# Expert layers: gates applied by one VectorE multiplication per group, normalised one group later

## The reference

```python
def peer_ffn(x, norm_g, q_w, sub_keys, u, v):
    h = rmsnorm(x, norm_g).reshape(T, D)
    q = (h @ q_w).reshape(T, PEER_HEADS, 2, PEER_HALF)
    s = jnp.einsum('thcd,ckd->thck', q, sub_keys)
    s1, i1 = lax.top_k(s[:, :, 0], PEER_TOPK)          # 16 of 128 keys
    s2, i2 = lax.top_k(s[:, :, 1], PEER_TOPK)
    cand_s = s1[..., :, None] + s2[..., None, :]
    best_s, best_pos = lax.top_k(cand_s, PEER_TOPK)    # 16 of 256 pairs
    gate = jax.nn.softmax(best_s, axis=-1)
    a = jnp.einsum('nd,nhkd->nhk', hb, u[ib])          # dot with the gathered row of u
    w = gb * jax.nn.gelu(a, approximate=False)
    return jnp.einsum('nhk,nhkd->nd', w, v[ib])        # sum of the gathered rows of v
```

## Time and profile before

| | |
|---|---|
| median of 3 runs | 2998.92 us (2991.95 to 3008.18) |
| the profiled execution | 2997.89 us, its span 2996.1 us |
| DVE / ACT / PE / POOL busy | 56% / 39% / 85% / 32% of the span |
| first expert layer, first gather to last value matmul | 1414.4 to 2092.2 us |
| second expert layer, the same | 2269.0 to 2946.2 us |
| DMA in most of both | 418 GB/s |

### The profile page before, as it was taken

How to read it: one execution, slowest core, us unless ns; L and a number is a source line. 1 busy time by engine, 2 the same in 40 slices (tenths; PEclk the granted TensorE clock), 3 DMA queues, 4 the chain that set the end, 5 groups by cost and what they waited for, 6 DMA issues and landing times.

```text
span 2996.1 us, 35285 instructions
## 1 busy us (share of the span) xinstructions
PE 2532.5 (85%) x11858; PEld 1798.1 (60%) x11858; DVE 1685.7 (56%) x3591; ACT 1172.0 (39%) x2504; POOL 946.0 (32%) x736
## 2 busy tenths in 40 slices
PE   7999899999789999858888878787877887788787
PEld 7988699899669979737544333233755443333334
DVE  4551355555465534672566766665365666677663
ACT  4446544434464346423333232323453332323233
POOL 0005400000230048226444333332525443333343
PEclk9999999999899999879999999999888999989998
DMA  5553255455325545204999999998417999999993
GB/s 190 183 170 120 96 190 182 165 182 185 107 92 182 189 156 185 68 28 158 393 410 406 422 421 419 419 413 341 155 57 290 416 408 419 421 420 421 414 415 151
DMA packets 141950, 783.39 MB, mean 261 GB/s; under 512 B 15872, under 2 KB 16384, under 8 KB 76288
## 3 DMA queue, kind: packets, MB, share of 16 engines
q0 software_dynamic: 73728, 536.90, 43.5%
q1 hardware_dynamic: 65360, 237.44, 23.6%
q10 hardware_dynamic: 2736, 7.46, 0.8%
HBM read 780.69 MB, written 1.05 MB: 261 GB/s over the span
## 4 chain that ended last, share of the span: by engine, by line
PE 45%; DMA 21%; issue 10%; DVE 10%; POOL 7%; ACT 6%; POOLq 0%; SPq 0%; DVEq 0%; ACTq 0%
DMA arena<-experts,arena 21%; PE ps L451 12%; PE ps L452 11%; PE ps L453 11%; POOL ring_lo L312 5%; PE ps L892 5%; PE ps L895 4%; DVE arena L1908 4%; ACT row L1307 2%; POOL arena L2013 1%; ACT arena L1300 1%; DVE ring_lo L312 1%; DVE arena L1426 0%; DVE hT_lo L1492 0%; POOL rs L1992 0%
## 5 line engine op out<-in xcount | busy, mean ns | idle before, releaser
L892 PE MATMUL ps<-arena,row 128*128 128x512 f32 x1024 | 576.7, 647 | 219.4 <-ACT row L1307 219.3
L1908 DVE SCALAR_TENSOR_TENSOR arena<-arena,ps 128x1024 f32<-128x1024 f32 x512 | 612.1, 1219 | 263.1 <-DMA arena<-experts,arena 263.0
L2013 POOL DMA_INDIRECT arena<-experts,arena x512 | 487.1, 951 | 735.2 <-PE ps L895 527.4
L451 PE MATMUL ps<-hT_hi,ring_hi 128*128 128x256 f32 x2048 | 597.2, 292 | 62.5 <-POOL ring_lo L312 56.5
L452 PE MATMUL ps<-hT_lo,ring_hi 128*128 128x256 f32 x2048 | 592.9, 289 | 0.0
L453 PE MATMUL ps<-hT_hi,ring_lo 128*128 128x256 f32 x2048 | 592.4, 289 | 0.0
L895 PE MATMUL ps<-arena,row 128*128 128x512 f32 x1024 | 559.4, 629 | 0.0
L306 ACT ACTIVATE ring_hi<-ring 128x1024 fp32r<-128x1024 f32 x448 | 462.8, 1057 | 168.9 <-PE ps L453 154.8
L312 POOL TENSOR_TENSOR ring_lo<-ring,ring_hi 128x1024 fp32r<-128x1024 f32 x180 | 433.9, 2418 | 294.0 <-ACT ring_hi L306 232.0
L892 PEld LDWEIGHTS ps<-arena,row 128*128 128x128 f32 x1024 | 198.0, 203 | 514.2 <-ACT row L1307 300.7
L451 PEld LDWEIGHTS ps<-hT_hi,ring_hi 128*128 128x128 f32 x2048 | 406.5, 199 | 71.6 <-issue 65.8
(11 more groups left out here) (261 smaller groups left out, 2941.2 us busy)
## 6 DMA issues: line engine op xcount, KB each, us to landing
ring<-stream SPq DMA_DIRECT2D x448, 512.0 KB, 3.7
arena<-experts,arena POOLq DMA_INDIRECT x512, 13.0
row<-rows_in ACTq DMA_DIRECT2D x11, 512.0 KB, 4.0
x<-x_in SPq DMA_DIRECT2D x1, 1024.0 KB, 5.1
out<-arena SPq DMA_DIRECT2D x2, 512.0 KB, 2.7
arena<-cols_in ACTq DMA_DIRECT2D x3, 256.0 KB, 2.6
cols<-cols_in SPq DMA_DIRECT2D x1, 425.5 KB, 5.6
arena<-cols_in ACTq DMA_DIRECT2D x1, 320.0 KB, 2.9
```

The lines of the kernel that those rows point to most:

```text
L451: pe.matmul(dst, a[0], b[0], start=start, stop=False)
L892: lower = pe.matmul(ps[:, 2 * tb, :], diag, v[:, 0:HALF], start=first, stop=end)
L1908: last = dve.scalar_tensor_tensor(u, u, 1.0, h, ALU.mult, ALU.mult, accum_out=R["a"][:, n % 2, k:k + 1])
L2013: pool.indirect_dma_start(R["held"][:, g % HELD, :], None, experts, bass.IndirectOffsetOnAxis(ap=idx[:, n % 2, k:k + 1], axis=0))\
```

## The change

ACT no longer scales the four numbers of a group. It applies Gelu, raises `peer_g` and waits for `peer_w`. DVE multiplies the group's four Gelu results with its four gates in one instruction (`gated`), which stands two dots into the **next** group (one dot in where that group has two picks, none where it has one), and raises `peer_w`; the layer's last group has its multiplication at the end. The three instructions of `gates(n)` move from the end of unit n - 1 to behind group 0 of unit n; those of unit 0 stay where they were.

```diff
                 def weights(n, group):
                     first, end = groups_of(n)[group]
                     act.wait_ge(of("peer_a"), group_count(l, n, group) + 1)
-                    act.wait_ge(of("peer_gate"), UNITS * l + n + 1)
-                    link(act.activation(R["g"][:, n % 2, first:end], R["a"][:, n % 2, first:end], ACT.Gelu))
-                    for k in range(first, end):
-                        last = act.activation(R["w"][:, n % 2, k:k + 1], R["g"][:, n % 2, k:k + 1], ACT.Copy,
-                                              scale=R["gate"][:, n % 2, k:k + 1])
-                    link(last)
+                    act.activation(R["g"][:, n % 2, first:end], R["a"][:, n % 2, first:end], ACT.Gelu)\
+                       .then_inc(of("peer_g"), 1)
+                    act.wait_ge(of("peer_w"), group_count(l, n, group) + 1)
                     taken = PICKS * l + TOPK * n + end - 2 * GROUP
...
+                def gated(n, group):
+                    first, end = groups_of(n)[group]
+                    dve.wait_ge(of("peer_g"), group_count(l, n, group) + 1)
+                    dve.wait_ge(of("peer_gate"), UNITS * l + n + 1)
+                    dve.tensor_tensor(R["w"][:, n % 2, first:end], R["g"][:, n % 2, first:end],
+                                      R["gate"][:, n % 2, first:end], ALU.mult).then_inc(of("peer_w"), 1)
+
                 def dots(n, group):
                     h = bank(4 + 2 * (n // PH), 2)
-                    for k in range(*groups_of(n)[group]):
+                    first, end = groups_of(n)[group]
+                    for k in range(first, end):
+                        if k == first + min(2, end - first - 1) and (n or group):
+                            gated(*((n, group - 1) if group else (n - 1, len(groups_of(n - 1)) - 1)))
...
                 for n in range(UNITS):
                     dots(n, 0)
+                    if n:
+                        gates(n)
                     if n + 1 < UNITS:
                         top_keys(n + 1)
...
                     for group in range(3, len(groups_of(n))):
                         dots(n, group)
-                    if n + 1 < UNITS:
-                        gates(n + 1)
...
+                gated(UNITS - 1, len(FINE) - 1)
                 add_piece(layer, in_banks, 1)
```

## The result

The changed kernel takes 3015.22 us (median of 20 runs, 2999.93 to 3021.69), the kernel before 3000.52 us in the same rounds (20 runs, 2991.95 to 3008.77). The ratio is 1.0039 with a 95% interval of 1.0028 to 1.0050. On 3000.5 us that is 11.7 us more, between 8.4 and 15.0; the two medians themselves stand 14.7 us apart. The forecast was 11.6 us more, said as 3010 us because the median known then was 2998.9.

What follows compares the result with a forecast made beforehand. The prediction took the gathers' DMA to bound the kernel, leaving only layer starts and ends open. Starts 8.6 plus ends 3.0 gave 11.6 us on 2997.9 us: 3009.5, said as 3010 us, range 2997 to 3024 us.

Steps and rivals of the forecast that it cites:

- The bound: In the picks' stretch DMA gathers limit the time, share 1.01 at 418 GB/s; only places with an empty queue are open.
- The starts, 4.3 us each: At each layer's start the twelfth gather goes out 4.3 us later and nothing makes up for it; 8.6 us in all.
- upper end: At the starts: 5.2 us per layer, if one pick more runs at half clock after TensorE's longer idleness.
- The ends, 1.5 us each: At each layer's end the weights of picks 8 to 11 follow pick 12's dot, 1.5 us later; 3.0 us in all.
- the upper bound: At the ends: 3.2 us each, if picks 4 to 7, also late, run at half clock into this point.
- The picks' stretch, 0: With the picks alone, later slots cost 0: gathers keep at least 7.9 us to land and need 5.2.
- ACT's list, 0: Work behind ACT's wait for the multiplication costs 0; beside queries the nearest gather has 10.9 us against 5.2 needed.
- The multiplication, 0.2 us hidden: On DVE, 66 multiplications per layer at 0.2 us, 26 us in all, hidden in its waits for landings.
- The gates, 0: Moving the gates removes 30 DVE waits of some 4.3 us; gain 0, at most 2 us per layer.
- Nothing is lost at the start: Rival: the start's queue is empty for another reason and the 4.3 us fall into it; 2998 to 3001 us, chance 0.16.
- DVE stands at the multiplication: Rival: beside the queries DVE waits for Gelu, delaying dots and indices; 16 to 32 us more, 3026 to 3042 us, chance 0.14.
- DVE's freedom pays: Rival: without 30 DVE waits, earlier indices keep the queue full; at most 10 us gained, 2988 us, chance 0.08.

Runs made afterwards that it cites:

- the first multiplication at once: Changed kernel, but group 0 of each layer's first unit multiplied directly behind its own dots; ratio to the kernel before 1.0022.
- unit 0's gates later: Changed kernel, with the gates of each layer's first unit behind its group 0 and the next unit's key search; ratio to before 0.9976.
- the three kernels with ACT's scalings: The kernel before, and it with gates moved behind group 0, without (0.9986) or with (0.9969) unit 0's gates behind the next key search.
- the gates alone: Kernel before, scalings still on ACT, only the gates of unit n moved behind its group 0; ratio to before 0.9986.
- four dots: Changed kernel, with every multiplication behind the last dot of the next group instead of its second; ratio to before 1.0897.
- three dots: Changed kernel, with the multiplication behind the third dot of the next group instead of the second; ratio to before 1.0284.
- the kernel that has it: Changed kernel, first unit's gates behind the next unit's key search, last unit's groups 1 to 5 multiplied at once; ratio to before 0.9967, median 2988.88 us.
- the kernel that has the scalings: Kernel before, gates moved behind group 0 and the first unit's behind the next unit's key search; ratio to before 0.9969, median 2988.18 us.
- the kernel with both places at once: Changed kernel, with group 0 of each layer's first unit and groups 1 to 5 of its last multiplied behind their own dots; ratio to before 1.0003.
- the kernel that multiplies everywhere at once: Changed kernel, with every group multiplied directly behind its own dots, DVE waiting there for Gelu; ratio to before 1.0064.

## Why the prediction was right

The places of the loss and the waits behind it are as forecast. That the size agrees to 0.1 us is luck: the interval spans 8.4 to 15.0 us, and the parts agree less well than their sum. In the profiled executions the layers are 6.2 and 3.4 us longer, where 5.8 each was forecast.

**The bound.** It held. In the picks' stretch the share stayed at 1.01 with 417 GB/s, and what the change lost lies where the queue is empty.

**The starts, 4.3 us each.** Measured 4.2 and 4.0 from the first dot, and 4.2 and 2.4 from the first gather, at the place named. The queue stands still for 7 us instead of 3 in the first layer. TensorE's start at half clock came as in the earlier trace rows, 2.07 us for the first pair, and no pick more ran slow: the gather is issued 4.06 us after TensorE starts, exactly as before (1447.51 to 1451.57, 1449.07 to 1453.13). The sum's middle value was right, and not its upper end. The 5.2 us that I took for a lone gather, with up to 1 us to its semaphore as a guess, is 5.38 and 5.41 in the changed kernel.

**The ends, 1.5 us each.** From last dot to last matmul it takes 1.5 us more in the second layer and 2.5 in the first. The timeline of the changed kernel at the end of the first layer, and then of the second:

```profile
2073.39 1.55 PE L892 MATMUL ps<-arena,row 128*128 128x512 f32 x2 [3.54 <-ACT row L1304]
...
2079.52 1.28 ACT L1304 ACTIVATE row<-cols,arena 128x128 f32<-128x128 f32 x4 [2.35 <-DVE arena L1903]
...
2079.93 0.19 PEld L892 LDWEIGHTS ps<-arena,row 128*128 128x128 f32 x1 [0.24 <-issue]
...
2934.43 1.28 ACT L1304 ACTIVATE row<-cols,arena 128x128 f32<-128x128 f32 x4 [2.39 <-DVE arena L1903]
...
2935.76 1.13 PE L892 MATMUL ps<-arena,row 128*128 128x512 f32 x2 [0.35 <-ACT row L1304]
```

In the second layer it is as I had it: TensorE stands 0.35 us until the diagonals of picks 8 to 11 are there, and runs to the end from then on. In the first it doesn't wait for them: at 2079.93 it is still busy with picks 4 to 7, which came late and began slowly at 2073.39. That is the upper bound's reason. Over all kernels the extra 1 us goes with a slow start of TensorE just there: where the last unit's groups are deferred, the six ends (of the changed kernel, of the first multiplication at once, and of unit 0's gates later) take 9.35, 8.28, 8.23, 7.69, 8.22 and 8.27 us, median 8.25. In the three kernels with ACT's scalings it is 6.81, 6.81, 8.48, 6.80, 6.78 and 6.79, median 6.8, and the 8.48 has a slow start too (the gates alone, 1.89 us for the first pair at 2076.96). The difference of the medians is 8.25 - 6.8 = 1.45 us, which is the 1.5 forecast.

**The picks' stretch, 0.** The cost is 0, but the slack was less than I worked out. I said that no gather would have under 7.9 us to land. The chain of the changed kernel, with pieces in order of time (start, duration, what):

```profile
1698.60 0.09 DVE arena L1903
...
1698.71 1.28 ACT row L1304 x4
...
1700.04 2.08 PE ps L892 x2
1702.12 1.72 PE ps L895 x2
...
1704.10 7.36 DMA arena<-experts,arena
```

It is 7.36 us here and 6.81 at 1644.44. One step that failed is the 2.3 us from TensorE's start to the first free slot. I took it from a group that began at full clock. This one begins at half and takes 4.06. Of the groups for which TensorE waited, 27 of 98 began slowly before (over 1.5 us for the first pair), 34 of 108 in the changed kernel, and 64 of 109 behind four dots. The other step is when the second dot is done: at 1644.44 the chain runs through DVE alone from a landing at 1631.28 to the multiplication at 1639.04, because DVE had the next unit's experts to find and a copy to make (line 1856) before these dots, and I had let the dots follow their landings. With 5.4 us for a gather alone, 6.81 - 5.4 = 1.4 us of slack were left where I thought 7.9 - 5.2 = 2.7. It didn't matter for two dots. One dot more takes 2.5 us off, more than the slack, which fits the 2.8% of three dots and is why I misjudged both variants.

**ACT's list, 0.** Beside the queries the share is 1.01 with 413 GB/s, and ACT's waits for TensorE's scores went down, from 129.9 us to 111.3. No cost shows.

**The multiplication, 0.2 us hidden.** It takes 0.163 us. With the starts and ends equal, the kernel that has it and the kernel that has the scalings take 0.9967 and 0.9969, so it is hidden, as the scalings were.

**The gates, 0.** As predicted: waits of 181 us turned into waits for landings. With the gates alone moved the interval [0.9972, 1.0001] leaves room for the small gain that was the bound.

**The rivals.** "Nothing is lost at the start" is refuted by the starts' 4 us and by the kernel with both places at once. "DVE stands at the multiplication" names a real mechanism, shown by the kernel that multiplies everywhere at once, but the two dots between dodge it. I had not named that distance as a reason against the rival. One of my signs of being wrong was a wait of DVE for Gelu of microseconds; taken by the letter it is there, 2.7 us at the longest, but 10.2 us in 12 waits is no cost that shows, and I had put the rival's threshold at 5. "DVE's freedom pays" did not come about by the 30 short waits. It does with the two long ones, which the change left in place: the kernels in which they are moved as well gain 7 to 10 us over the kernel before, and 10 was the limit that I had set for that rival.

## What to carry to other kernels

Measure a ring of buffers by the landings that are left when a slot may be let go, and compare that time with the whole way back to a landing. As long as it fits, moving a step later is free in the steady state, and once it doesn't, every turn pays: here two dots cost 0.4%, all of it at starts and ends, and three and four cost 2.8% and 9.0%. A step that is deferred for the steady state should still be done at once at both ends of the loop, where the queue is empty, and the group behind the first has to be looked at too, since the stall may only move there; and an engine that runs its list in order should not meet a long wait while work that has already landed stands behind it.

## What the runs showed of the hardware

A gather of 1.049 MB issued into an empty queue took 5.38 and 5.41 us from issue to landing (changed kernel, at 1453.13 and 2310.09), while in a full queue one lands every 2.5 us. If moving the data takes a lone gather those 2.5 us too, which is an estimate from the full queue, 2.9 us of its time are something else.

TensorE's granted clock fell back to 0.50 after short waits in the middle of the steady state. In the changed kernel the slow starts came after 1.83 us of idleness at the least (median 3.6), the quick ones after up to 4.17 us (median 1.4), so the length of the idle stretch alone does not decide. With the first multiplication at once the clock even fell between 1448 and 1450 while TensorE worked without a gap:

```profile
1448.00:1449.00 1.00, 1.00 (x3) 0.38 (x2) 0.97 (x6) 0.85 (x2) 0.00 (x0) 1.00 1.00 414
1449.00:1450.00 1.00, 1.00 (x3) 0.36 (x2) 0.96 (x3) 0.00 (x0) 0.00 (x0) 0.52 1.02 426
```

The Trainium skill (TensorE: Matmul & The Clock Gate, "What's actually happening") calls the throttled clock the default which activity lifts. The rows agree as to the starts at 0.50. What made this one fall a microsecond after the start is not settled by any run here.
